# Moving the low halves of all weight units from VectorE to GpSimd, and six turns from TensorE to VectorE

## What is computed

```python
def reference(...):
    # block 1
    proj = rms_norm(x, g_mix) @ w_in                 # c_q, c_kv, k_rope, dq, dk, dv
    ...                                              # MLA (8 heads), differential attention (4 heads)
    x = x + concat(out_mla, out_diff) @ w_out
    x = x + cross_attention(rms_norm(x, g_xattn), rms_norm(mem, g_mem))  # w_xq, w_xk, w_xv, w_xo
    h = rms_norm(x, g_ffn)
    x = x + (silu(h @ w_gate) * (h @ w_up)) @ w_down # hidden width 5632
    x = rms_norm(x, g_final)
    # block 2
    z = rms_norm(x, g_mix_2) @ w_in_2                # aq, ak, av, rq, rk, rv, rg
    ...                                              # MoBA attention (8 heads), retention (8 heads)
    x = x + concat(a_out, r_out) @ w_o_2
    h = rms_norm(x, g_ffn_2)
    x = x + (silu(h @ w_gate_2) * (h @ w_up_2)) @ w_down_2
    gate = sigmoid(rms_norm(x, g_ple_2) @ w_ple_gate_2 + b_ple_gate_2)
    return x + (p @ w_ple_proj_2) * gate
```

## Time and profile before

| | |
|---|---|
| median of 3 runs | 2437.94 us (2437.32 to 2438.88) |
| profiled execution, its own time | 2438.7 us |
| its span | 2436.7 us |
| mean granted TensorE clock | 0.999 of full |
| busy: TensorE, VectorE, ScalarE, GpSimd | 2415.9, 1503.1, 1146.5, 10.4 us |
| HBM read | 458.35 MB, 189 GB/s over the span |

### The profile page before, as it was taken

How to read it: one execution, slowest core, us unless ns; L and a number is a source line. 1 busy time by engine, 2 the same in 40 slices (tenths; PEclk the granted TensorE clock), 3 DMA queues, 4 the chain that set the end, 5 groups by cost and what they waited for, 6 DMA issues and landing times.

```text
span 2436.7 us, 31597 instructions
## 1 busy us (share of the span) xinstructions
PE 2415.9 (99%) x11112; PEld 2015.7 (83%) x11112; DVE 1503.1 (62%) x1812; ACT 1146.5 (47%) x1537; POOL 10.4 (0%) x23
## 2 busy tenths in 40 slices
PE   8999999999999999999999999999999999999999
PEld 7988878888888888888888888888888888888887
DVE  7766655667556665575666655557755666566565
ACT  6455555644434443445554445454433444344453
POOL 0000000000000000000000000000000000000000
PEclk9999999999999999999999999999999999999999
DMA  8645445465555655565555565555555555556554
GB/s 312 211 166 172 167 163 173 158 205 192 190 196 190 193 193 191 190 194 187 178 184 192 187 200 167 187 187 189 192 196 194 193 191 191 197 180 204 187 182 163
DMA packets 125992, 461.96 MB, mean 190 GB/s; under 512 B 14000, under 2 KB 14128, under 8 KB 125120
## 3 DMA queue, kind: packets, MB, share of 16 engines
q1 hardware_dynamic: 123360, 446.75, 55.5%
q0 software_dynamic: 2384, 13.68, 1.6%
q10 hardware_dynamic: 144, 0.07, 0.0%
HBM read 458.35 MB, written 2.10 MB: 189 GB/s over the span
## 4 chain that ended last, share of the span: by engine, by line
PE 98%; DVE 1%; DMA 1%; ACT 1%; issue 0%; SPq 0%; ACTq 0%; DVEq 0%
PE acc L448 92%; PE acc L453 2%; PE pt L512 2%; PE acc L617 1%; PE po L663 1%; DMA raw<-stream 1%; PE po L655 1%; PE pt L634 0%; DVE w_lo L1195 0%; ACT w_hi L789 0%; PE acc L601 0%; DVE mix_lo L1504 0%; ACT tmp_b L943 0%; ACT mix_hi L1004 0%; DVE mix_lo L1519 0%
## 5 line engine op out<-in xcount | busy, mean ns | idle before, releaser
L1195 DVE TENSOR_TENSOR w_lo<-raw,w_hi 128x1024 fp32r<-128x1024 f32 x844 | 1026.4, 1224 | 821.8 <-ACT w_hi L789 814.0
L789 ACT ACTIVATE w_hi<-raw 128x1024 fp32r<-128x1024 f32 x844 | 894.0, 1060 | 1149.3 <-PE acc L448 1108.0
L448 PE MATMUL acc<-w_hi,norm_hi 128*128 128x512 f32 (+1 forms) x2240 | 873.7, 390 | 0.0
L448 PE MATMUL acc<-w_hi,norm_lo 128*128 128x512 f32 (+1 forms) x2240 | 868.8, 388 | 0.0
L448 PE MATMUL acc<-w_lo,norm_hi 128*128 128x512 f32 (+1 forms) x2240 | 596.1, 388 | 0.0
L448 PEld LDWEIGHTS acc<-w_hi,norm_lo 128*128 128x128 f32 x2240 | 420.6, 188 | 85.0
L448 PEld LDWEIGHTS acc<-w_hi,norm_hi 128*128 128x128 f32 x2240 | 420.5, 188 | 84.9
L448 PEld LDWEIGHTS acc<-w_lo,norm_hi 128*128 128x128 f32 x2240 | 419.4, 188 | 86.3
L448 PE MATMUL acc<-w_hi,mix_hi 128*128 128x512 f32 x1088 | 428.2, 394 | 5.3 <-ACT w_hi L789 3.9
L448 PE MATMUL acc<-w_hi,mix_lo 128*128 128x512 f32 x1088 | 425.0, 391 | 0.0
L448 PE MATMUL acc<-w_lo,mix_hi 128*128 128x512 f32 x1088 | 290.9, 389 | 0.0
(11 more groups left out here) (200 smaller groups left out, 859.2 us busy)
## 6 DMA issues: line engine op xcount, KB each, us to landing
raw<-stream SPq DMA_DIRECT2D x844, 512.0 KB, 3.4
x<-x_tok POOLq DMA_DIRECT2D x2, 2048.0 KB, 9.5
heads<-x_in POOLq DMA_DIRECT2D x4, 512.0 KB, 6.4
x<-mem_tok POOLq DMA_DIRECT2D x2, 1024.0 KB, 5.7
heads<-rows_in POOLq DMA_DIRECT2D x2, 1024.0 KB, 6.5
heads<-decay_in POOLq DMA_DIRECT2D x4, 512.0 KB, 5.5
heads<-mem_in SPq DMA_DIRECT2D x3, 512.0 KB, 9.9
out<-x SPq DMA_DIRECT2D x3, 512.0 KB, 5.3
```

Of the source, the lines that this page charges most:

```text
L448: last = pe.matmul(acc[:, slot, c * NB:c * NB + width], a[:, k * T + c * P:k * T + (c + 1) * P], w[:, s, kk * width:(kk + 1) * width], sta ...
L789: act.activation(w_hi[:, (units.fixed - 1) % RING, :], src, ACT.Copy).then_inc(w_hi_ready, 1)
L1195: dve.tensor_tensor(w_lo[:, s, :], src, w_hi[:, s, :].bitcast(F32), ALU.subtract)\
```

## The change

1. GpSimd makes all 844 low halves (`low`, a tensor_tensor as VectorE's was). Its 19 transfers stand between them: `until(n)` makes low halves up to unit n, with a loop where it can, and then comes the wait and the transfer.
2. VectorE has no splits left; `during` only runs the inserted work in order, with the waits that it had.
3. In both MLPs TensorE no longer turns down blocks 0 to 2 of the last group. VectorE turns them with 16 STREAM_TRANSPOSE each into tmp_c (x_turned), ScalarE makes norm_hi from tmp_c and VectorE norm_lo.
4. GROUPS is (3, 4, 4), so that the last group's down blocks have 8 units.
5. ScalarE waits before each set of squares until its own last one is done (squared_last).

```diff
-GROUPS = (4, 4, 3)
+GROUPS = (3, 4, 4)
...
+        x_turned = sem("x_turned")
...
         def _(pool):
+            units = Tally()
+
+            def low(s):
+
+                pool.wait_ge(w_hi_ready, units.add())
+                pool.tensor_tensor(w_lo[:, s, :], raw[:, s, :], w_hi[:, s, :].bitcast(F32), ALU.subtract)\
+                    .then_inc(raw_read, 1)
+
+            def until(end):
+
+                while units.fixed < end and units.fixed % RING:
+                    low(units.fixed % RING)
+                n = (end - units.fixed) // RING
+                if n > 1:
+                    with turns(pool, n, {units: RING}):
+                        for s in range(RING):
+                            low(s)
+                while units.fixed < end:
+                    low(units.fixed % RING)
...
+            until(2)
             pool.wait_ge(mem_landed[1], 16)
             pool.dma_start(con[:, :], consts).then_inc(con_landed, 16)
             pool.dma_start(pos[:, TT:].bitcast(I32), positions).then_inc(con_landed, 16)
-
             pool.wait_ge(mem_landed[NBD], 16)
             for b in range(NBD):
-                pool.wait_ge(raw_read, 2 * (b + 1))
+                until(2 * (b + 1))
                 pool.dma_start(block_of(heads, X_IN // CB + b), block_of(x_in, b)).then_inc(x_landed[b], 16)
+            until(U_X + RING)
             pool.wait_ge(block_taken, 1)
...
+            until(first_mlp + RING)
             pool.wait_ge(head_split, MLA_H + X_H)
             load_row(G_ROW, ROWS.index("g_final"), final_landed)
...
+            until(UNITS)
...
                     if g == len(GROUPS) - 1:
-                        residual(nd, mix, need=down, first={TURN_AT: turn_hidden}, turned=turned)
+                        for b in range(NBD):
+                            one_block(nd, mix, token_major=True, need=down, mid=None if b else {TURN_AT: turn_hidden})
+                        operands.add(NBD - 1)
...
+            def squared_last():
+
+                if squares.fixed:
+                    act.wait_ge(squares_ready, squares.fixed)
+                squares.add()
...
                         if b == 0:
                             last_hidden_hi(n - 1)
-                        elif last:
-                            turned_hi(b - 1, next_name)
                         split(2)
                         if last and beside and b == NBD - 1:
                             beside()
-                        split(nd - 4)
+                        split(1)
+                        if b and last:
+                            act.wait_ge(x_turned, squared_turns.add())
+                            hi_gained(tmp_c[:, :], norm_hi, b - 1, next_name)
+                        split(nd - 5)
                         if last:
                             wait_taken()
-                            token_squares(x_of(b), 0, b, tmp_c)
+                            token_squares(x_of(b), 0, b, tmp_a)
...
-            def during(n, at=None):
-
-                for i in range(n):
-                    split(1)
-                    if at and i in at:
-                        at[i]()
+            def during(at):
+
+                for i in sorted(at):
+                    at[i]()
...
                     for b in range(NBD):
-                        split(2)
-                        if b == 0:
-                            hidden_low(n - 1, both_pt)
-                        split(1)
                         if b and last:
-                            turned_low(b - 1, next_name)
-                        split(1)
...
+                            if final:
+                                dve.wait_ge(final_ready, b)
+                            rows_ = by_tile(block_of(heads, Y // CB + b - 1)) if final else x_of(b - 1)
+                            for quarter in range(4):
+                                turned = turn_quarters(rows_, (quarter,))
+                            turned.then_inc(x_turned, 1)
+                            if beside and b == NBD - 1:
+                                beside()
+                            low_gained(tmp_c[:, :], (norm_hi, norm_lo), b - 1, next_name)
+                        else:
+                            if b == 0:
+                                hidden_low(n - 1, both_pt)
                         take_added(nd, b)
```

More of the change, by code:

```diff
@@ L372, in _, with load_row @@
         def _(pool):
+            units = Tally()
[13 more added lines that the diff above has]
+                    low(units.fixed % RING)
+            def load_row(first, row, landed):
+                pool.dma_start(heads[:, first * T:first * T + D],
+                               rows_in[row:row + 1].broadcast_to([P, D])).then_inc(landed, 16)
+            until(2)
             pool.wait_ge(mem_landed[1], 16)
@@ L564, in output, with mlp @@
                     one_block(NU, mix, token_major=True, mid={TURN_AT: turn_x(b - 1)})
-            def mlp(need, turned):
+            def mlp(need):
                 for g, n in enumerate(GROUPS):
@@ L722, in _ @@
             residual(CB // UK, mix, need=lambda ki: (head_split, MLA_H + UK * (ki + 1)))
-            mlp(need, turn_final)
+            mlp(need)
             need = operand_need(operands.fixed - (NBD - 1))
@@ L765, in _ @@
         def _(act):
-            raws, units, taken, rows, turned, hidden, finals, norms = (Tally() for _ in range(8))
+            raws, units, taken, rows, turned, hidden, squared_turns, finals, norms, squares = (Tally() for _ in range(10))
             job = [0]
@@ L837, in block_squares @@
             def block_squares(dst, junk, parts, width, scale=None):
+                squared_last()
                 act.wait_ge(w_used, units.value(RING - 1))
@@ L1173, in _ @@
         def _(dve):
-            raws, units, ends, taken, his, squared, sums, roots_n, funcs, rows, own, rotated = (
-                Tally() for _ in range(12))
+            ends, taken, his, squared, sums, roots_n, funcs, rows, own, rotated = (
+                Tally() for _ in range(10))
             def link(ins):
@@ L1338, in mlp, with turn_quarters @@
             def mlp(name, next_name, final=False, aside=None, beside=None):
-                def turn_hidden(quarters):
+                def turn_quarters(rows, quarters):
                     for to in quarters:
@@ L1352, in up @@
                 def up():
-                    split(1)
-                    split(NU - 1)
                     take_times(NU, tmp_b, tmp_a)
-                    split(1)
                 for g, n in enumerate(GROUPS):
@@ L1360, in mlp @@
                     if g == 0:
-                        column_norm(name, NU)
+                        column_norm(name)
                         dve.sem_inc(rows_ready, 1)
                         rows.add()
-                    else:
-                        split(NU - 1)
                     gate()
@@ L1369, in mlp @@
                     up()
-                    with turns(dve, n - 1, {units: 2 * NU, raws: 2 * NU, ends: 2 * NU, taken: 2, funcs: 1,
-                                            his: 1}) as i:
-                        split(1)
+                    with turns(dve, n - 1, {ends: 2 * NU, taken: 2, funcs: 1, his: 1}) as i:
                         turn_hidden(range(2))
-                        split(1)
                         turn_hidden(range(2, 4)).then_inc(hidden_turned, 1)
-                        split(3)
                         hidden_low(i, tmp_c[:, :])
-                        split(NU - 6)
                         gate()
@@ L1382, in mlp @@
                     for b in range(NBD):
-                        split(2)
-                        if b == 0:
-                            hidden_low(n - 1, both_pt)
-                        split(1)
                         if b and last:
-                            turned_low(b - 1, next_name)
-                        split(1)
-                        if last and beside and b == NBD - 1:
-                            beside()
-                        split(nd - 5)
+                            if final:
[10 more added lines that the diff above has]
+                                hidden_low(n - 1, both_pt)
                         take_added(nd, b)
@@ L1528, in _ @@
                 mem_low(i)
-                split(n)
             dve.wait_ge(sums_done, sums.add())
@@ L1814, in _ @@
             b = NBD - 1
-            split(NU)
             dve.wait_ge(tile_used, 1)
@@ L1823, in _ @@
                 dve.tensor_tensor(x_of(b)[:, t, :], x_of(b)[:, t, :], gated, ALU.add).then_inc(out_ready, 1)
-            assert units.fixed == UNITS and raws.fixed == UNITS
 def weight_units(w, columns=None):
```

82 lines of the change are left out of this document (35 added, 47 removed).

## The result

The changed kernel took 2496.27 us (median of 4 runs, 2495.20 to 2497.36) against 2438.14 for the kernel before beside it (4 runs, 2437.32 to 2438.88): 1.0238 of the time, interval 1.0225 to 1.0251. The forecast was 2460, with 2495 as its upper end. The sign was right and 36 us of the loss were missing. The profiled execution, 2496.41 us, is the one read here.

A forecast was written before the change was run, and what follows sets the result against it. TensorE, busy 2415.9 of 2436.7 us, was taken as the bound. Terms -5.2 - 1.4 - 1.0 + 0.4 + 21.6 + 4.4 + 3.0 = +21.8 us on 2438.7 gave 2460.5, by the runs' median 2460; range 2427 to 2495.

The forecast's parts named there:

- Low half on GpSimd: Each low half on GpSimd takes 2.28 us (1.06 to 3.18), hidden while below TensorE's 2.72 us per unit.
- GpSimd is not the bound: Denies a rival: low halves above 2.72 us each, waits included, make GpSimd the bound, over 100 us slower; chance 12%.
- Holding by whole instructions: Likeliest case: VectorE instructions with both operands in SBUF and GpSimd's low halves wait for each other entirely; chance 46%.
- term 6: VectorE and GpSimd holding each other: +21.6 us in rotate_normed, +4.4 at the first MLP's end, +3.0 in differential heads.
- No holding: Rival: both engines run beside each other or slow each other within slack, -8.5 us, 2429.4 us; chance 42%.
- Term 4: Start: low halves three and four queue behind GpSimd's wait for mem_in, TensorE 2.9 us late, mostly regained: +0.4 us.
- Term 6, rotations: Four rotate_normed: VectorE's instructions alternate with low halves, TensorE waits 5.4 us each time: +21.6 us.
- Term 6, end of the first MLP: Last group's down blocks: norm_lo from tmp_c is held, w_hi 2.2 us late in each of two blocks: +4.4 us.
- Term 6, heads: Differential attention's probabilities are held: +3 us, bounds 0 and 10; MLA and MoBA heads: nothing.
- Term 1: Both MLPs: six turns leave TensorE at 0.87 us each, 5.2 us less.
- Term 2: First output product: mix_lo no longer stands behind a low half on VectorE, 1.4 us less; the 1.30 us stall kept.
- Term 3: Cross-attention: no low half in front of the first maximum any more, about 1.0 us less.

The follow-up runs named there:

- rotate_psum: Changed kernel with the four rotate_normed's three products reading acc in PSUM instead of tmp_c in SBUF (scale per head left out): 2467.5 us, one run.
- pool_writes: Changed kernel with GpSimd's subtraction replaced by a memset of w_lo to zero, so it reads nothing; waits and places stay: 2426.16 us, one run.
- dve_start: Changed kernel with the low halves of the first 40 units back on VectorE, GpSimd making the rest: 2471.87 us, one run.
- pool_start: Changed kernel with GpSimd making only low halves of units 0 to 39, 96 to 119 and both MLPs from their ninth unit, VectorE the others: 2452.78 us, 1.0058.
- turns_only: Changed kernel with every low half back on VectorE, the six turns still off TensorE: 2432.92 us, 0.9977 of the kernel before.
- pool_mlp: Changed kernel with GpSimd making only the low halves of both MLPs from their ninth unit (512), VectorE the others: 2432.51 us, 0.9977 of the kernel before.
- pool_mlp5: Repetition with more runs of the kernel of pool_mlp: 2432.67 us, 0.9978 of the kernel before.

## Why the prediction was right or wrong

- **Low half on GpSimd.** 2.28 forecast, 2.45 measured in the mean and 2.40 undisturbed: right, and GpSimd is not the bound. The estimate worked out from the Trainium skill's "GPSIMD Engine Reference" (Performance versus the Vector engine), 2.25 us, is 6% low against 2.40.
- **Holding by whole instructions** (term 6) is right as a mechanism, and "No holding" is refuted by rotate_psum and pool_writes. The Trainium skill's "SBUF — State Buffer" (Who interferes with whom) states this rule; the trace agrees for instructions with two operands in SBUF (477 ns with one of them in PSUM, 2394 in the mean with none), and for GpSimd that only writes (480 ns). Its price was called an upper end, one low half for each instruction, and is none: 16.20 us for one norm_lo, over seven low halves.
- **Term 4, the start, is the step that failed**: +0.4 forecast, +21.8 measured. It priced where GpSimd's third low half stands, and put at nothing the holding that term 6 had just adopted. VectorE's list has mix_lo and sixteen norm_lo from heads there, then the scaling of the tables and the first rotation, all inside SBUF and with TensorE waiting behind them. dve_start and pool_start show that the low halves of these forty units make the loss, and pool_writes that the same list loses nothing there when GpSimd only writes. Term 6's own price for the sixteen norm_lo, 16 x (2.28 + 0.48) = 44 us, is near the measured 37.2 by luck: one of them takes almost half of it, and eight take no longer than before.
- **Term 6, rotations**: 5.4 forecast for each, 6.6 measured. The instructions alternated with low halves there, as forecast (the text says four of them and lists five; five is right). The idle time was less than forecast (4.5 us before each of the four turns), but the turn and the matmuls behind it then ran slowly. That cost had no term.
- **Term 6, end of the first MLP**: 4.4 forecast, 5.0 measured, in another place. The forecast had w_hi late in two blocks; it was Y late before the last turn.
- **Term 6, heads**: 3 forecast for the differential heads (bounds 0 to 10), 6.9 measured; MoBA's at nothing, 3.3 measured.
- **Term 1**: 5.2 forecast, 4.7 measured in turns_only, but given back in the changed kernel: what turned the blocks on VectorE also moved norm_lo's operand from PSUM into SBUF.
- **Term 2**: the first output product gained 3.2 where 1.4 was forecast. **Term 3**: the cross-attention's 1.0 did not come (+1.3). Why is not shown; two traces of one kernel (pool_mlp, pool_mlp5) differ by 0.8 us in this part.
- **The range**: its upper end, 2495, is 1.3 us short, and that it came so near is luck. The bounds that the text names (28 + 4.4 + 10 + 5 for term 6) give 2478; MoBA's heads have no number, and the start has no bound at all. A third of term 6 gives 2440, not 2443.

## What to carry to other kernels

Before work with two inputs goes to GpSimd, list every VectorE instruction with both operands in SBUF, and every scaling or copy inside SBUF, over the whole program, however short. What matters is which of them TensorE waits for. Count at least one GpSimd instruction for each, and where GpSimd has several ready one behind the other, count that one instruction can stand over all of them. Then give GpSimd the stretches that have none (here 536 of 844 low halves, 0.9964 of the time) and leave the rest where it was, or put one operand of the waited-for instruction into PSUM. Moving an operand from PSUM into SBUF is a change too. And look at the single instructions of a held group: its mean hid all of this.

## What the runs showed of the hardware

Holding does not depend on size: a product of 128x8 took 2.14 us (L1743 above) where it took 0.17. How long it lasts differs. From 61.5 us on, seven norm_lo and seven low halves alternated one for one, 2.6 us each; at 43 us one norm_lo stood for 16.20 us while GpSimd went from low half to low half. In both cases GpSimd had no idle time between its instructions (two transfer issues stood between them in the second). From 164 us on no VectorE instruction of the changed kernel took over 3.5 us. What lets VectorE in between two low halves is open.

After an idle stretch of 4.5 us TensorE comes back at its lower level of 1.2 GHz. The changed kernel around the first rotated turn (length, TensorE, weight loads, VectorE, ScalarE, GpSimd, granted clock):
```profile
1244.20:1248.70 4.50, 0.05 (x1) 0.00 (x0) 4.44 (x2) 1.06 (x1) 4.50 (x3) 1.00 0.51 177
1248.70:1252.20 3.50, 3.48 (x13) 3.09 (x14) 0.00 (x0) 1.02 (x1) 2.18 (x1) 0.53 0.51 162
1252.20:1262.00 9.80, 9.80 (x45) 8.11 (x44) 0.07 (x1) 4.40 (x19) 4.80 (x2) 0.99 0.36 111
```
The granted clock is 0.53 over 3.5 us, and the turn takes 1.97 us instead of 1.04. The turn's matmuls and those behind it are what this stretches: each of the four idle stretches costs about 2 us more than it lasts, which is the 6.6 against 4.5 of the rotations. The start has the same level: 0.50 over 2.8 us behind the 5.20 us of waiting for mix_lo.

Reading and writing hold different things. GpSimd's reading held instructions with two operands in SBUF and its memset did not (685 ns against 2880); the memset held scalings and copies inside SBUF (0.96 us against 0.47).
